# Latent attention of the second block: queries by kind of column, and the out projection's first half between the attention's steps

## The reference

```python
cq, ckv, kr = ...                       # 384, 256 and 32 columns of xn @ w_in
qh  = (rmsnorm(cq, mla_q_norm) @ w_uq).reshape(B, S, 8, 96)          # 64 plain + 32 rotated columns per head
q   = concat([qh[..., :64], rope(qh[..., 64:], positions)])
kvh = (rmsnorm(ckv, mla_kv_norm) @ w_ukv).reshape(B, S, 8, 128)      # 64 key + 64 value columns per head
k   = concat([kvh[..., :64], broadcast(rope(kr), 8 heads)])
mla_out = mla_causal(q, k, kvh[..., 64:])                            # softmax over causal blocks of 128 queries
return concat([ret_out, mla_out]) @ w_o                              # 512 + 512 rows of w_o, 1024 columns
# second_block: h = h + rmsnorm(mix, post_mix_norm); hn = rmsnorm(h, pre_ffn_norm); ff = ...
```

## Time and profile before

| | us |
|---|---|
| timed runs, median of 3 | 2135.41 (2135.29 to 2136.5) |
| profiled execution, its own time | 2133.75 |
| its span | 2131.9 |
| TensorE busy | 1804.3 (85% of the span) |
| VectorE busy | 778.7 (37%) |
| ScalarE busy | 695.8 (33%) |
| GpSimd busy | 71.6 (3%) |
| mean granted TensorE clock | 0.95 |

### The profile page before, as it was taken

How to read it: one execution, slowest core, us unless ns; L and a number is a source line. 1 busy time by engine, 2 the same in 40 slices (tenths; PEclk the granted TensorE clock), 3 DMA queues, 4 the chain that set the end, 5 groups by cost and what they waited for, 6 DMA issues and landing times.

```text
span 2131.9 us, 35498 instructions
## 1 busy us (share of the span) xinstructions
PE 1804.3 (85%) x14296; PEld 1227.9 (58%) x14296; DVE 778.7 (37%) x1472; ACT 695.8 (33%) x1284; POOL 71.6 (3%) x176
## 2 busy tenths in 40 slices
PE   6988999788777777777787777699979899999988
PEld 5854888544344344343443443388657678788866
DVE  4447225622222222222222223544563533332254
ACT  3347322232222222222222222432464522222151
POOL 0000000000000000000000003400000000000000
PEclk9999999899999999999999999899989999999999
DMA  5430122689999999999999999642212132334210
GB/s 187 126 99 2 60 99 99 233 352 429 425 425 427 425 427 426 425 428 426 426 427 425 428 425 426 247 132 69 78 35 70 50 109 79 99 99 138 99 60 40
DMA packets 106898, 505.41 MB, mean 237 GB/s; under 512 B 9128, under 2 KB 56488, under 8 KB 73552
## 3 DMA queue, kind: packets, MB, share of 16 engines
q1 hardware_dynamic: 98720, 490.49, 57.4%
q10 hardware_dynamic: 7248, 11.37, 2.0%
q0 software_dynamic: 864, 2.64, 0.4%
HBM read 497.31 MB, written 2.11 MB: 234 GB/s over the span
## 4 chain that ended last, share of the span: by engine, by line
PE 57%; DMA 28%; DVE 6%; ACT 5%; issue 3%; SPq 1%; ACTq 0%; DVEq 0%
DMA ring<-in_w 27%; PE bank L582 13%; PE bank L583 12%; PE bank L584 12%; PE bank L1954 8%; PE bank L1866 4%; PE bank L1945 3%; ACT w_hi L660 2%; DVE w_lo L673 1%; PE bank L739 1%; PE bank L763 1%; PE bank L751 1%; DMA raw<-in_w_in 1%; SPq L1602 1%; PE bank L1043 0%
## 5 line engine op out<-in xcount | busy, mean ns | idle before, releaser
L1954 PE MATMUL bank<-ring,XTs 128*32 128x256 f32 x4096 | 290.0, 431 | 115.4 <-DMA ring<-in_w 112.2
L2169 DVE TENSOR_TENSOR x<-x,bank 128x512 f32<-128x512 f32 x264 | 163.9, 682 | 488.4 <-PE bank L1945 488.4
L673 DVE TENSOR_TENSOR w_lo<-raw,w_hi 128x2048 fp32r<-128x2048 f32 (+3 forms) x83 | 183.2, 2208 | 382.7 <-ACT w_hi L660 382.3
L582 PE MATMUL bank<-hTh,w_hi 128*128 128x512 f32 (+1 forms) x720 | 286.2, 397 | 20.5 <-ACT arena L1481 11.1
L1954 PEld LDWEIGHTS bank<-ring,XTs 128*32 128x32 f32 x4096 | 144.1, 121 | 263.0 <-issue 206.0
L583 PE MATMUL bank<-hTh,w_lo 128*128 128x512 f32 (+1 forms) x720 | 283.6, 394 | 0.0
L584 PE MATMUL bank<-hTl,w_hi 128*128 128x512 f32 (+1 forms) x720 | 282.3, 392 | 0.0
L660 ACT ACTIVATE w_hi<-raw 128x2048 fp32r<-128x2048 f32 (+3 forms) x83 | 152.8, 1843 | 215.3 <-PE bank L584 206.8
L1963 PE MATMUL bank<-ring,aT 128*32 128x256 f32 x2048 | 123.8, 382 | 89.6 <-DVE aT L2189 89.6
L582 PEld LDWEIGHTS bank<-hTh,w_hi 128*128 128x128 f32 (+1 forms) x720 | 135.5, 188 | 59.2 <-issue 21.2
L1779 ACT ACTIVATE y<-bank 32x256 f32<-32x256 f32 x256 | 96.1, 376 | 223.8 <-PE bank L1945 136.7
(11 more groups left out here) (375 smaller groups left out, 2215.6 us busy)
## 6 DMA issues: line engine op xcount, KB each, us to landing
ring<-in_w SPq DMA_DIRECT2D x192, 2048.0 KB, 19.6
raw<-in_w_in SPq DMA_DIRECT2D x25, 1024.0 KB, 5.4
raw<-in_w_gate SPq DMA_DIRECT2D x11, 1024.0 KB, 5.4
raw<-in_w_up SPq DMA_DIRECT2D x11, 1024.0 KB, 5.3
raw<-in_w_down SPq DMA_DIRECT2D x11, 1024.0 KB, 4.9
raw<-in_w_out SPq DMA_DIRECT2D x4, 1024.0 KB, 5.1
raw<-in_w_o SPq DMA_DIRECT2D x4, 1024.0 KB, 5.0
raw<-in_w_ple_gate SPq DMA_DIRECT2D x4, 1024.0 KB, 5.0
```

What stands on the lines that cost most here:

```text
L582: pe.matmul(dst, left[0], right[0], start=start, stop=False)
L673: ins = v.tensor_tensor(lo, src, hi, ALU.subtract)
L1954: mm = pe.matmul(Hb[BLK * j:BLK * (j + 1), :], XTs[u][:, 4 * (c % 2) + 2 * h + c // 2, :], w[:, at_:at_ + Q], start=(h == 0 and c == 0), s ...
L2169: ins = v.tensor_tensor(xs, xs, Sb[t % 2][n][:, :], ALU.add)
```

## The change

- **Queries by kind of column.** The parts of `w_uq` are laid out with the plain columns of four heads first (256) and then their rotated columns (128). Each unit gives three jobs of 128 rows instead of four of 96: one with the rotated rows of four heads, two with the plain rows of two heads each. ScalarE copies the rotated job to `mq_r` (128 partitions), and swaps halves with eight DMAs of 16 partitions; VectorE turns four heads at once, three operations over 128 by 512. GpSimd's queue then issues four DMAs per unit that put the rotated rows into `mqT` (`spread`). Plain rows are copied head by head (`two_heads`). The parts of `w_uq` and `w_ukv` are now made in two instructions per unit.
- **Order ahead of the attention.** TensorE: three jobs of unit 0, the rotated job of unit 1, `ret_b`, the two plain jobs of unit 1, keys, values. VectorE turns unit 0's queries, then the keys, then makes the low part of `w_ukv`; the four splits of the retention stand between its multiplications. The key rows go out in two DMAs of four heads each.
- **Banks of the second attention.** Scores use banks 0 and 1 at every step (one step at a time), transposes 2 and 3, results 4 and 5. Banks 6 and 7 are free for the out projection.
- **Out projection in two parts.** Its units are now `or0`, `or1` (the retention's rows) and `om0`, `om1` (the attention's rows). The `or` products, 96 matmuls, stand between the steps of the attention, 6 after each of the iterations 0 to 15; ScalarE copies their results to `mixg`. The `om` products follow the attention, tile by tile; VectorE adds the two halves from PSUM, and the norms of a tile follow.
- **Parts of weights.** Both `or` units are split before VectorE's attention begins, `om0` inside it, `om1` after it, and the first `w_gate` unit after the last norm (its part buffer is `om0`'s, in use until the last tile).

```diff
-        plan("mq", ML_H)
+        for k in range(2):
+            J["mq_r"] += bk.take(1)
+            if k == 1:
+                plan("ret_b", RH)
+            J["mq_n"] += bk.take(2)
...
-            J[name + "_s"] = [[bk.take(1, (2 * (t % 2) + s,))[0] for s in range(2)] for t in range(steps)]
+            J[name + "_s"] = [[bk.take(1, (s if room else 2 * (t % 2) + s,))[0] for s in range(2)] for t in range(steps)]
...
+        for n in range(2):
+            J[f"or{n}"] = bk.take(NT, (6, 7))
+            ends(f"or{n}")
...
+            read(pe, J["mv"])
             pe.wait_ge(S("ret_out"), RH)
...
+            def pe_between():
...
+                for n in range(2):
+                    u = units_of[f"or{n}"][0]
+                    for i, job in enumerate(J[f"or{n}"]):
+                        loaded(pe, u)
+                        wh, wl = parts(u)
+                        claim(pe, job)
+                        rows_ = slice(P * i, P * (i + 1))
+                        for c in range(4):
+                            mm = three(pe, banks[job.bank][:, :], (catT[0](c)[:, rows_], catT[1](c)[:, rows_]),
+                                       (wh[:, c, :], wl[:, c, :]), c == 0, c == 3)
+                            if c == 1:
+                                yield
+                        fill(mm, job)
+                        yield
...
+            stretches = pe_between()
+            pe_attention(pe, MLA, lambda t: next(stretches, None))
...
+            read(pe, J["mla_v"])
+            for i in range(NT):
...
+                for n in range(2):
+                    u, job = units_of[f"om{n}"][0], J[f"om{n}"][i]
+                    loaded(pe, u)
...
+            def turned(k):
+                v.wait_ge(S(f"mq_swapped{k}"), 128)
+                dve_rope(v, chain, mq_r[k], mq_swap[k], cos3, sin3).then_inc(S("mq_roped"), 1)
...
+            turned(0)
...
             lo_until(v, units_of["ukv"][0].n)
-            rope_queries(0)
-            rope_queries(1)
...
+                if h:
+                    dve_split(v, ("ret", h - 1), ofTl[:, h - 1, :], rqT[:, h - 1, :], ofTh[:, h - 1, :]).then_inc(S("ret_out"), 1)
...
+            turned(1)
+            lo_until(v, units_of["or0"][0].n)
+            lo_until(v, units_of["or1"][0].n)
...
+            dve_attention(v, MLA, chain, lambda t: next(stretches, None))
...
+            lo_until(v, units_of["om1"][0].n)
...
+                for n in range(2):
+                    job, cols = J[f"om{n}"][i], slice(512 * n, 512 * (n + 1))
+                    full(v, job)
+                    read(v, J[f"or{n}"][i:i + 1])
+                    free(v.tensor_tensor(mixo[:, i, cols], mixg(i)[:, cols], banks[job.bank][:, :], ALU.add), job)
+                read(v, [J["om0"][i], J["om1"][i]])
+                chain(v.tensor_tensor(mixg(i), mixo[:, i, :], gain_mix, ALU.mult))
...
             normed(NT - 1)
+            lo_until(v, units_of["gate"][0].n)
             dve_split_jobs(v, "hT4", hTh, hTl, lambda c: PRM("pre_ffn", c))
...
             queries(0)
+            two_heads(J["mq_n"][0], mqT, 0, -(ML_QK ** -0.5))
+            two_heads(J["mq_n"][1], mqT, 1, -(ML_QK ** -0.5))
+            hi_until(act, units_of["ukv"][0].n)
             queries(1)
...
+            key_rows(0)
+            two_heads(J["mk"][0], mkT[0], 0, 1.0)
+            two_heads(J["mk"][1], mkT[0], 1, 1.0)
             act.wait_ge(S("ret_out"), RH)
...
+            hi_until(act, units_of["or1"][0].n)
...
+            act_attention(act, MLA, lambda t: next(stretches, None))
...
+            hi_until(act, units_of["om1"][0].n)
...
+            def spread(k):
+                pool.wait_ge(S("mq_roped"), k + 1)
+                for i in range(4):
+                    pool.dma_start(mqT[ML_N:ML_QK, 4 * k + i, :], mq_r[k][ML_R * i:ML_R * (i + 1), 0, :])\
+                        .then_inc(S(f"mq_there{k}"), 16)
```

More of the change, by code:

```diff
@@ L347, in build @@
         stationary("ukv", a["w_ukv_2"][0], 0, ML_H * (ML_N + ML_V), 1024)
-        units_of["ukv"][0].by_kind = True
-        for n in range(2):
-            moving(f"o{n}", a["w_o_2"][0], 512 * n, 512)
+        units_of["ukv"][0].kinds = (ML_N, ML_V)
+        for u in units_of["uq"]:
+            u.kinds = (ML_N, ML_R)
+        for part, lo in (("or", 0), ("om", 512)):
+            for n in range(2):
+                unit(f"{part}{n}", cols_of(a["w_o_2"][0][lo:lo + 512, :], 512 * n, 512 * (n + 1)), 4, 512)
         n_ff = DFF // 256
@@ L395, in plan, with ends @@
                         u.part = n_part[0]
+        def ends(name):
+            us = units_of[name]
+            for k, u in enumerate(us):
+                u.last = J[name][(k + 1) * len(J[name]) // len(us) - 1]
         plan("hT1", DC)
@@ L442, in build @@
         plan("ckvT", KVL // P)
[L443 to L446 removed]
+        J["mq_r"], J["mq_n"] = [], []
+        for k in range(2):
[3 more added lines that the diff above has]
+            J["mq_n"] += bk.take(2)
+            units_of["uq"][k].last = J["mq_n"][-1]
         plan("mk", ML_H // 2)
@@ L802, in act_attention, with dve_attention @@
                     act_split(act, (A.name, p), A.out(p)[0], banks[A.jv[p].bank][:, :])
-        def dve_attention(v, A, chain):
+                if between and t:
+                    between(t - 1)
+        def dve_attention(v, A, chain, between=None):
             for t in range(A.n + 4):
@@ L1505, in act_second, with act_between @@
                 free(act.activation(mv[:, i, :], banks[job.bank][:, :], ACT.Copy), job)
-            hi_until(act, units_of["o0"][0].n)
-            act_attention(act, MLA)
-            hi_until(act, units_of["o0"][1].n)
+            hi_until(act, units_of["or1"][0].n)
+            def act_between():
+                for n in range(2):
+                    for i, job in enumerate(J[f"or{n}"]):
+                        ahead(hi_until, act, f"or{n}", i)
+                        yield
+                        full(act, job)
+                        free(act.activation(mixg(i)[:, 512 * n:512 * (n + 1)], banks[job.bank][:, :], ACT.Copy), job)
+                        yield
+            stretches = act_between()
+            act_attention(act, MLA, lambda t: next(stretches, None))
+            for _ in stretches:
+                pass
+            hi_until(act, units_of["om1"][0].n)
             read(act, J["mla_v"])
@@ L1511, in act_second @@
             n5, n6 = TileNorm("n5"), TileNorm("n6")
-            for n in range(2):
-                ahead(hi_until, act, f"o{n}")
-                for i, job in enumerate(J[f"o{n}"]):
-                    full(act, job)
-                    if n == 0 and i == 0:
-                        read(act, J["mla_v"])
-                    free(act.activation(mixo[:, i, 512 * n:512 * (n + 1)], banks[job.bank][:, :], ACT.Copy), job)
-                    if n == 1:
-                        read(act, [J["o0"][i], job])
-                        n5.act(act, i, mixo[:, i, :], av(12288, D), ssq, rstd)
-                        if i:
-                            act.wait_ge(S("x3"), i)
-                            n6.act(act, i - 1, x[:, i - 1, :], av(12288, D), ssq2, rstd2)
+            for i in range(NT):
+                read(act, [J["om0"][i], J["om1"][i]])
+                n5.act(act, i, mixo[:, i, :], av(12288, D), ssq, rstd)
+                if i:
+                    act.wait_ge(S("x3"), i)
+                    n6.act(act, i - 1, x[:, i - 1, :], av(12288, D), ssq2, rstd2)
             act.wait_ge(S("x3"), NT)
             n6.act(act, NT - 1, x[:, NT - 1, :], av(12288, D), ssq2, rstd2)
+            hi_until(act, units_of["gate"][0].n)
             act_split_jobs(act, "hT4", hTh, lambda c: PRM("pre_ffn", c))
```

184 lines of the change are left out of this document (101 added, 83 removed).

## The result

| | before | after |
|---|---|---|
| timed runs, median | 2135.95 us (2135.29 to 2137.29) | 2120.64 us (2119.38 to 2123.76), 4 runs |
| ratio | | 0.9930 [0.9913, 0.9947] |
| profiled execution, its own time | 2133.75 | 2120.2 |
| its span | 2131.9 | 2118.4 |
| TensorE busy | 1804.3 | 1803.1 |

The changed kernel is 15.3 us faster, where 8.6 were forecast; 2120.64 lies under the range of 2121.5 to 2131.5. The sign came out, and so did the chain of waits at the front and in the tail; the size did not, most of all in the attention.

A forecast was written before the change was run, and what follows sets the result against it. TensorE was taken as the long engine, with ScalarE's and VectorE's order setting four holes. A 9.1 us gain less 0.5 of clock gave 8.6: 2133.75 to 2125.1 profiled, plus 1.66 for the median, 2126.8 us; range 2121.5 to 2131.5.

The forecast's parts named there:

- Queries and their turning: Ahead of the attention: 54 query matmuls for 72, minus 4.1 us; VectorE's turning 4.1 us instead of 14.6.
- Second scores: Attention's start: TensorE's second scores need VectorE's first score done, so start at about 1568.4, 43.1 us after the first query matmul.
- The attention: Second scores to attention's end: 47.1 us from before, plus 0.7 and 21.0, minus 3.4 of waits for ScalarE: 65.4 us.
- Out projection: The rest after the attention: last split, 12 matmuls, a 0.7 us wait and 84 matmuls, 24.5 us in sum.
- Norms and tail: Out projection's end to first gate matmul: norms keep step but for about 1 us; 11.7 us, 14.0 before.
- Gate to `w_up`: Feed-forward's start: first `w_up` matmul 7.2 us after the first gate matmul, 7.31 before.
- The low clock that I feared at the feed-forward's start: Some 3 us of idle ahead of the first gate matmul lowers TensorE's clock: between 0 and 3.4 us, 0.5 taken.
- 1 (score banks): Attention: TensorE waits each step for VectorE to take both heads, 1.3 us times 15 = 19.5; 2146.3 us, chance 0.06.
- 2 (ScalarE's queue): Front: DMA issues, swaps and copies push second scores back to 1572.9, losing 4.5 us; 2131.3 us, chance 0.12.
- 3 (low clock): Attention and feed-forward's start: more half clock, 6.4 us lost at worst, 2 to 3 as a middle; 2129.5 us, chance 0.14.
- 4 (copies close up): Front: copies and splits close up, TensorE starts its attention 3 us earlier, norms keep step; 2122.5 us, chance 0.13.

The follow-up runs named there:

- `queries_only`: The kernel before with only the new queries and new order ahead of the attention, old out projection, banks and norms kept: 2127.60 us, ratio 0.9961.
- `or1_late`: The changed kernel with the second unit of the retention's rows split inside the attention instead of ahead of it: 2120.81 us, ratio 0.9931.
- `warm`: The changed kernel with eight unused matmuls in TensorE's 4.00 us hole ahead of the first scores: 2120.08 us, ratio 0.9926.
- `before_dense`: The kernel before with four unused matmuls in TensorE's waits at the attention's start: 2133.07 us, ratio 0.9988.
- `keys_pool`: `pool_swaps` with both swaps ahead of both spreads on GpSimd and VectorE turning the queries last: 2115.01 us, ratio 0.9902.
- `pool_swaps`: The changed kernel with the queries' sixteen swap DMAs issued from GpSimd's queue instead of ScalarE's: 2122.67 us, ratio 0.9938.

## Why the prediction was wrong in size

I take its steps in order, counted to the first `w_up` matmul: forecast 151.9 us, measured 146.2.

**Queries and their turning**: right in kind. The eight issues cost 5.24 us, forecast at 4.65 from two in 1.16, so ScalarE's copies began later than forecast. But the wait ahead of the keys was 4.20 for the forecast 4.2, and later copies and high parts closed up: the values were copied 1.4 us sooner. `queries_only` gave 7.5.

**Second scores**: 41.7 instead of 43.1, all of that 1.4. The reason was half right: `or0`'s low part and six matmuls at the low clock end at the same place as VectorE's first score (`or1_late`, `warm`).

**The attention**: this is the step that failed. I wrote "The low clock there is in the 47.1" and "I assume the same again", and so charged the changed kernel with the loss that before had. From the second scores to the end it took 62.0 us instead of 65.4, which is 3.4 less. The clock is 2.1 of them: `before_dense` shows 2.8 us of loss in before, `warm` 0.7 in after.

The other 1.3 are the price of a wait. I took away the idle time of the waits for ScalarE, 3.4 us, but a wait costs more than that. Before has the scores of 256 columns once without and once with a wait behind them:

```profile
1582.57 1.13 PE L739 MATMUL bank<-arena 96*128 96x256 f32 x4
1583.53 1.04 PE L751 MATMUL bank<-cst,arena 128*128 128x128 f32 x8
...
1593.32 1.13 PE L739 MATMUL bank<-arena 96*128 96x256 f32 x4
1594.91 1.09 PE L751 MATMUL bank<-cst,arena 128*128 128x128 f32 x8 [0.46 <-ACT arena L798]
```

From start to start it is 0.96 and 1.59 us, and the transposes are 0.05 longer: 0.68 us for a traced wait of 0.46, because without the wait the two groups' records overlap by 0.17. Before has seven waits with 4.1 us of idle time in this stretch, after one with 0.4; six waits less are 3.7 + 6 x 0.22 = 5.0 us, where I had taken 3.4. That is 1.6 more than forecast; the second step's scores, 0.86 us at full clock for the forecast 0.7, take 0.2 back, which leaves 1.4 for the 1.3.

A stretch of six matmuls takes 1.50 us and not the forecast 1.4, but it makes the scores behind it 0.10 us shorter (0.71 to 0.61 at 128 columns), so that its net cost is as forecast. It is the same 0.10 us at another place: the first matmul behind value products is longer, whichever it is. In after that is the stretch's own first:

```profile
1581.28 0.50 PE L604 MATMUL bank<-w_hi,ofTh 128*128 128x512 f32 x1
1581.62 0.40 PE L605 MATMUL bank<-w_hi,ofTl 128*128 128x512 f32 x1
...
1582.79 1.03 PE L768 MATMUL bank<-arena 96*128 96x256 f32 x4
```

A pair of heads confirms both prices: before's take 10.76 us with one wait and 11.43 with two. Less 0.68 per wait, plus 4 x (1.50 - 0.10), both give 15.7; measured are 15.68 for each in after.

**Out projection**: 24.7 for 24.5, right.

**Norms and tail**: 11.0 instead of 11.7. The last tile's `xn6` ends 7.0 us after the out projection (7.7 forecast); the splits follow as described. The tail is 14.0 - 11.0 = 3.0 us shorter than before's, and 3.4 shorter than in `queries_only`.

**Gate to `w_up`**: 6.9 for 7.2. The low clock that I feared at the feed-forward's start did come:

```profile
1667.00:1670.50 3.50, 3.46 (x10) 2.79 (x11) 3.50 (x6) 3.48 (x5) 0.00 (x0) 0.59 0.90 267
```

That is (1.00 - 0.59) x 3.46 = 1.4 us, but it stands wholly under the wait for `w_up`'s low part, which was 1.48 us before and is gone. So the 0.5 us charged for it was too much. From the first gate matmul to the end the profiles take 451.3 to 453.9 us, before 452.9.

The sum: 1.4 + 3.4 - 0.2 + 0.7 + 0.3 = 5.6 of the 5.7 us. In the profiled execution a start 2.4 us later hides part, and 1.6 more come behind `w_up`; 5.7 - 2.4 + 1.6 = 4.9 is what lies between the forecast 2125.1 and 2120.2. The medians show 6.2 (2126.8 to 2120.64); 1.2 more, because I added the 1.66 by which before's median stood above its profiled execution, and for after that is 0.44.

The rivals: 1 (score banks) is refuted for this kernel, and without the cover its four waits have 2.0 us of idle time in all, where it priced 19.5; what is dear there is mostly the clock. No row gave the 0.3 us "for the semaphores" in its price. 2 (ScalarE's queue) is refuted as a loss; the queue would be next to bind once VectorE's order is changed. 3 (low clock) went the other way: less clock was lost, not more. 4 (copies close up) is what happened at the front, 1.4 us of the 3 it named, with norms that keep step; I gave it 0.13.

What stays open: how the 5.0 us between one and two steps of score banks would fall with the clock held at 1.00, and why the clock stays low for longer in one of the two; whether VectorE's order alone gives half of `keys_pool`; and what holding both ends of the second scores at once, `warm` and `or1_late` together, would give.

## What to carry to other kernels

When a stretch of before is taken over as a lump, look at the granted clock inside it first: a low clock that meets dense matmuls costs half of the time that it lasts, one that meets a wait costs nearly nothing, and a change of order moves it from the one to the other. Short stretches of independent matmuls between dependent steps pay more than the traced waits (0.68 us for one of 0.46 here), and they cover a halved number of banks. Where an edit on one engine's order gives nothing, look in the rows for a longer chain that ends at the same place, and change that one as well.

## What the runs showed of the hardware

- Four matmuls of which nothing is used made a kernel 2.6 us faster (`before_dense`); the granted clock in the 7.2 us behind them went from 0.58 to 1.00.
- The first matmul behind the value products is 0.10 us longer than the others of its kind: scores of 128 columns take 0.71 us there and 0.61 behind products of 128x512, a product 0.50 and 0.39.
- A wait of TensorE costs more than the idle time in its row: 0.68 us from start to start where the row says 0.46.
- Eight DMA issues held ScalarE's queue 5.24 us, 0.65 each; on GpSimd's queue the same eight took 3.94 us, 0.49 each (row below, of `pool_swaps`). From issue to landing the first eight took 3.6 us (median) from ScalarE and 4.5 from GpSimd; the second eight 2.1 and 1.9. So neither queue lands them sooner both times. The Trainium skill (DMA: Bandwidth & Descriptors, Rules for kernel authors) says that spreading DMAs over several engines does not help their bandwidth and only saves issue time; here saving the issue time gave nothing by itself (`pool_swaps`) and came with 6.3 us where VectorE's order was changed too (`keys_pool`).

```profile
1533.57 3.94 POOL L965 DMA_DIRECT2D scratch<-scratch  x8 [141.11 <-ACTq L1567]
```
